# Two heads at a time: scores and values of a pair sent alternately in five attention stages

## What is computed

```python
rel = relu(einsum('bthd,bsd->bths', q_idx, k_idx)); score = einsum('bths,bth->bts', rel, w)   # index scores
logits = einsum('bthd,bshd->bhts', q, k) * scale        # DSA, MLA (qk over 64 + 32), MOBA, plus a bias or distance
logits = q @ k * scale + (c_q - c_k)                    # FOX, c = cumsum(log_sigmoid(f))
out = softmax(masked(logits)) @ v
# stick-breaking
z = q @ k * scale; log_1m = where(past, -softplus(z), 0)
w = where(past, exp(log_sigmoid(z) + reverse_exclusive_cumsum(log_1m)), 0); out = w @ v
```

## Time and profile before

| what | us |
| --- | --- |
| median of three runs | 1319.16 |
| lowest, highest | 1313.72, 1322.42 |
| span of the profiled execution | 1318.1 |
| PE busy | 1229.3 (93%) |
| POOL busy | 819.7 (62%) |
| ACT busy | 580.8 (44%) |
| DVE busy | 559.8 (42%) |

### The profile page before, as it was taken

One profiled execution on the slowest core, in us unless ns is written; L12 is line 12 of the kernel. 1 busy time (PEld: TensorE's weight loads), 2 busy tenths in 40 slices (PEclk: granted clock), 3 DMA queues, 4 the chain that ended last, 5 costly groups with the idle time before them and its releaser, 6 DMA issues.

```text
span 1318.1 us, 21658 instructions
## 1 busy us (share of the span) xinstructions
PE 1229.3 (93%) x8127; PEld 1083.5 (82%) x8127; DVE 559.8 (42%) x1133; ACT 580.8 (44%) x868; POOL 819.7 (62%) x286
## 2 busy tenths in 40 slices
PE   6898887999998879989999998999999998999996
PEld 2898686999996765779999968878899997899995
DVE  4368576655558573466223372133211043311113
ACT  0442433554542432435444525344578452544442
POOL 2666345888884520468888835545465677788884
PEclk9898887999999885789999998899999999899998
DMA  9698266999994240468556522524444545466552
GB/s 345 227 321 249 67 214 216 317 307 305 309 302 161 71 127 0 134 202 267 178 181 186 175 86 75 159 66 127 128 129 129 158 154 168 151 187 188 183 185 78
DMA packets 253065, 237.66 MB, mean 180 GB/s; under 512 B 17979, under 2 KB 216368, under 8 KB 253008
## 3 DMA queue, kind: packets, MB, share of 16 engines
q1 hardware_dynamic: 237312, 202.80, 49.6%
q10 hardware_dynamic: 14784, 31.98, 6.8%
q0 software_dynamic: 912, 2.09, 0.4%
HBM read 235.79 MB, written 1.05 MB: 180 GB/s over the span
## 4 chain that ended last, share of the span: by engine, by line
PE 74%; DVE 10%; DMA 5%; ACT 4%; POOL 4%; issue 2%; SPq 0%; DVEq 0%; POOLq 0%; ACTq 0%
PE bank L1125 17%; PE bank L1126 17%; PE bank L1127 17%; POOL unit_lo L679 3%; PE bank L1150 3%; PE bank L1152 2%; PE bank L1164 2%; PE bank L1277 2%; PE bank L1299 2%; ACT unit_hi L781 2%; DMA raw<-in_ev_w_in 2%; PE bank L1291 1%; PE bank L1196 1%; DVE x L1682 1%; PE bank L1280 1%
## 5 line engine op out<-in xcount | busy, mean ns | idle before, releaser
L679 POOL TENSOR_TENSOR unit_lo<-raw,unit_hi 128x2048 fp32r<-128x2048 f32 (+4 forms) x88 | 348.5, 3962 | 322.3 <-ACT unit_hi L781 322.2
L1125 PE MATMUL bank<-h_hi,unit_hi 128*128 128x256 f32 x1248 | 353.6, 283 | 0.0
L1126 PE MATMUL bank<-h_lo,unit_hi 128*128 128x256 f32 x1248 | 353.1, 283 | 0.0
L1127 PE MATMUL bank<-h_hi,unit_lo 128*128 128x256 f32 x1248 | 353.1, 283 | 0.0
L713 POOL TENSOR_TENSOR unit_lo<-raw,unit_hi 128x2048 fp32r<-128x2048 f32 (+1 forms) x70 | 257.3, 3675 | 85.8 <-ACT unit_hi L904 70.6
L1125 PEld LDWEIGHTS bank<-h_hi,unit_hi 128*128 128x128 f32 x1248 | 239.2, 192 | 4.1 <-issue 1.4
L1126 PEld LDWEIGHTS bank<-h_lo,unit_hi 128*128 128x128 f32 x1248 | 239.2, 192 | 2.7
L1127 PEld LDWEIGHTS bank<-h_hi,unit_lo 128*128 128x128 f32 x1248 | 239.2, 192 | 0.0
L781 ACT ACTIVATE unit_hi<-raw 128x2048 fp32r<-128x2048 f32 (+4 forms) x98 | 163.1, 1664 | 99.5 <-PE bank L1127 42.2
L716 POOL TENSOR_TENSOR down<-raw_down,down 128x1024 fp32r<-128x1024 f32 x70 | 168.4, 2406 | 0.0
L1789 DVE SCALAR_TENSOR_TENSOR work<-bank,cols,work 128x254 f32<-128x254 f32 (+1 forms) x176 | 72.7, 475 | 171.8 <-ACT work L891 171.8
(11 more groups left out here) (302 smaller groups left out, 2200.1 us busy)
## 6 DMA issues: line engine op xcount, KB each, us to landing
raw<-in_ffn_w_up SPq DMA_DIRECT2D x88, 512.0 KB, 5.2
raw<-in_w_in SPq DMA_DIRECT2D x60, 512.0 KB, 4.7
raw_down<-in_ffn_w_down SPq DMA_DIRECT2D x44, 512.0 KB, 4.9
raw<-in_w_up SPq DMA_DIRECT2D x64, 256.0 KB, 3.1
raw_down<-in_w_down SPq DMA_DIRECT2D x32, 512.0 KB, 3.5
raw<-in_ev_w_in SPq DMA_DIRECT2D x28, 512.0 KB, 5.2
ada<-in_ada_w ACTq DMA_DIRECT2D x13, 1024.0 KB, 6.6
att<-in_ada_w SPq DMA_DIRECT2D x12, 1024.0 KB, 7.7
```

What stands on the lines that cost most here:

```text
L679: nc.gpsimd.tensor_tensor(ul[g % 2][:, w], raw[g % 2][:, w], uh[g % 2][:, w].bitcast(F32), ALU.subtract).then_inc(lo_up, 1)
L1125: nc.tensor.matmul(o, sh, mh, start=first, stop=False)
L1126: nc.tensor.matmul(o, sh, ml, start=False, stop=False)
L1127: return nc.tensor.matmul(o, sl, mh, start=False, stop=last)
```

## The change

The ten steps over heads become four steps over pairs, in the index scores, the four softmax attentions and stick-breaking, on PE, ACT and DVE alike. `scores` sends the 128-column product of both heads, then the 256-column product of both; the rotary and bias products follow after those, alternately too. `weighted` sends the first product of both heads, then the second of both. Fillers are spread by `halves`: before the transposes of a pair and between the transposes and the values. Index scores use four banks instead of three. No product, no copy and no load is added or dropped.

```diff
-            turn(("idx", h), h % 3)
+            turn(("idx", h), h % 4)
...
+        FILL = {DSA: [[(G_BG[0], 0), (G_BG[0], 1)], [(G_BG[1], 0)], [(G_BG[1], 1)], [], [], [], [], []],
+                MLA: [[(None, 0), (None, 1)], [], [], [], [], [], [], []],
+                FOX: halves(G_QKV[MOBA], (3, 1, 2, 1, 2, 1, 1, 1)), MOBA: halves(G_QKVS, (3, 1, 2, 1, 2, 1, 1, 1)),
+                "stick": halves(G_GATE[:10], (3, 2, 3, 2, 3, 2, 3, 2))}
+
+        DONE = {a: [[g for g, part in fill if part == 1] for fill in f] for a, f in FILL.items()}
+        DONE[DSA] = [[], [], [G_BG[0]], [], [G_BG[1]], [], [], []]
+        DONE[MLA] = [[], [], [0, 1], [], [2], [], [3], []]
...
+                for h in range(4):
+                    exps(a, h)
+                for g in DONE[a][0]:
+                    filler(g)
+                for p in range(PAIRS):
+                    for h in (2 * p, 2 * p + 1):
+                        evac_pt(a, h)
+                    for g in DONE[a][2 * p + 1]:
                         filler(g)
+                    if p:
+                        out_high(a, p - 1)
+                    if p + 2 < PAIRS:
+                        for h in (2 * p + 4, 2 * p + 5):
+                            exps(a, h)
+                    if p + 1 < PAIRS:
+                        for g in DONE[a][2 * p + 2]:
+                            filler(g)
...
+            def scores(a, p):
+
+                heads = (2 * p, 2 * p + 1)
+                o = [begin(("score", a, h)) for h in heads]
+                q, k = qT(ATT_SET[a])[:, p, :], kT(ATT_SET[a])[:, p, :]
+                one = a in (DSA, MOBA)
                 for tt, (c0, n) in enumerate(((0, P), (P, S))):
...
+                    for i in range(2):
+                        r = slice(DH * i, DH * (i + 1))
+                        mm = nc.tensor.matmul(o[i][:, c0:c0 + n], q[r, P * tt:P * (tt + 1)], k[r, 0:n],
+                                              start=one or tt == 0, stop=one)
...
+                for tt, (c0, n) in enumerate(((0, P), (P, S)) if not one else ()):
+                    for i, h in enumerate(heads):
+                        if a == MLA:
+                            r0 = D_ROPE * (h % 4)
+                            mm = nc.tensor.matmul(o[i][:, c0:c0 + n], qrT[r0:r0 + D_ROPE, h // 4, P * tt:P * (tt + 1)],
...
+            def weighted(a, p, t, set_):
+
+                o, v = begin(("pv", a, p)), vv(set_)
+                for i in range(2):
+                    nc.tensor.matmul(o[DH * i:DH * (i + 1), 0:S], v[:, 0, DH * (2 * p + i):DH * (2 * p + i + 1)], t[i][:, 0:S],
+                                     start=True, stop=False)
+                for i in range(2):
...
+                scores(a, 0)
+                scores(a, 1)
+                for p in range(PAIRS):
+                    for g, part in FILL[a][2 * p]:
                         filler(g, part)
+                    for h in (2 * p, 2 * p + 1):
+                        transpose_p(a, h)
+                    for g, part in FILL[a][2 * p + 1]:
+                        filler(g, part)
...
+                    for h in (2 * p, 2 * p + 1):
+                        evacuated(pe, ("tr", a, h))
+                    weighted(a, p, PT, ATT_SET[a])
+                    if p + 2 < PAIRS:
+                        scores(a, p + 2)
...
+                for h in range(4):
+                    soft(a, h)
+                for h in range(2):
+                    normalize(a, h)
+                for p in range(PAIRS):
+                    for h in (2 * p + 2, 2 * p + 3) if p + 1 < PAIRS else ():
+                        normalize(a, h)
+                    for h in (2 * p + 4, 2 * p + 5) if p + 2 < PAIRS else ():
+                        soft(a, h)
+                    if p:
+                        out_low(a, p - 1)
                     if between:
```

More of the change, by code:

```diff
@@ L461, in leave, with halves @@
                 self.base, self.k = self.start + iterations * per, 0
[L464 to L473, removed]
+        PAIRS = HEADS // 2
+        def halves(units_, counts):
+            parts = iter([(g, part) for g in units_ for part in range(2)])
+            return [[next(parts) for _ in range(n)] for n in counts]
+        FILL = {DSA: [[(G_BG[0], 0), (G_BG[0], 1)], [(G_BG[1], 0)], [(G_BG[1], 1)], [], [], [], [], []],
[5 more added lines that the diff above has]
+        DONE[MLA] = [[], [], [0, 1], [], [2], [], [3], []]
         MOD_PE = (2, 3)
@@ L854, in attention @@
             def attention(a, filler):
[L855 to L862, removed]
-                        filler(g)
-                out_high(a, HEADS // 2 - 1)
+                for h in range(4):
[6 more added lines that the diff above has]
+                    for g in DONE[a][2 * p + 1]:
+                        filler(g)
+                    if p:
[6 more added lines that the diff above has]
+                            filler(g)
+                out_high(a, PAIRS - 1)
             def load_rows(a, *srcs):
@@ L1943, in _, with dsa_between @@
             unit_evacuated(dve, G_CX[-1])
-            def dsa_between(st):
-                for g in DONE[DSA].get(st, []):
+            def dsa_between(p):
+                for g in G_BG[p:p + 1]:
                     i = g - G_BG[0]
@@ L2048, in _, with mla_between @@
             dve.wait_ge(lat_lo, 3)
-            def mla_between(st):
-                i = st % 2
-                if st in (2, 3):
+            def mla_between(p):
+                for i in range(2) if p == 0 else ():
                     dve.wait_ge(pool_mixed, i + 1)
@@ L2061, in mla_between @@
                     ins.then_inc(pool_scaled, 1)
-                if st in (4, 5):
+                for i in range(2) if p == 1 else ():
                     dve.wait_ge(pool_hi, i + 1)
@@ L2089, in _ @@
             attention(MOBA)
-            for st in range(HEADS + 2):
-                if st < HEADS:
-                    h = st
+            for p in range(PAIRS):
+                heads = (2 * p, 2 * p + 1)
+                for h in heads:
                     o = full(dve, ("z", h))
@@ L2108, in _ @@
                     V.tensor_tensor(wT[h % 2], zm[h % 2], o[:, 0:384], ALU.subtract).then_inc(free(("sfx", h)), 1)
-                if st >= 2 and st % 2 == 1:
-                    out_low("stick", (st - 2) // 2)
+                if p:
+                    out_low("stick", p - 1)
+            out_low("stick", PAIRS - 1)
             for c in range(4):
```

151 lines of the change are left out of this document (61 added, 90 removed).

## The result

The changed kernel takes 1270.85 us (median of four runs, 1265.59 to 1272.92) against 1319.44 for the kernel before in the same session; the ratio is 0.9612, 95% interval 0.9585 to 0.964. In a second session it took 1267.62 (ratio 0.959, 0.9574 to 0.9606). By the first ratio the time is 0.9612 x 1319.16 = 1268 us. Forecast were 1281, range 1270 to 1300, so the gain was larger than expected and the time just past the edge of the range; the interval of the ratio, 1264 to 1272 us, takes in that edge. The profiled executions differ by more, 1318.1 - 1263.5 = 54.6 us: the changed kernel's is the fastest of its four. The kernel before comes in two groups: of 19 later executions 7 took 1313.2 to 1315.6 us at a mean granted clock of 0.946 to 0.950, the other 12 took 1320.5 to 1325.1 at 0.937 to 0.941, so single profiles of it can differ by some 7 us.

The account below looks back on a forecast made before the run. PE, with 74% of the chain, was taken as the bound, in DSA and MLA also VectorE's and ScalarE's order. Terms 0 - 7.3 - 12.2 - 8.0 - 5.6 - 5.0 = -38.1 took 1319.2 to 1281 us, range 1270 to 1300.

Parts of the forecast that it names:

- The walk through ScalarE: DSA: ScalarE's late evacuations make PE wait 2.9 and 5.7 us; the stage ends at 166.2 against 173.5, -7.3 us.
- The forecast's cover: Index scores: PE's saved 0.85 us falls before a 4.84 us wait ended by VectorE's top-k chain; counted 0.
- MLA: MLA stage: pairs overlap, 32-row products too, with W waiting on ScalarE; ends at 532.7 against 544.9, -12.2 us.
- then the low clock as now: MLA: scores of pairs 0 and 1 take 2.07 us each at full clock, later ones 3.73 at the low clock.
- the last rival (0.06): More than forecast: DSA's waits shrink and MLA's clock rises, time below 1272 us; chance 0.06.
- FOX: FOX stage: scores save 4.2 us, values 3.2, a shorter low clock 0.6, waits 0; sum -8.0.
- The term of 0.6: Start of FOX: the low clock shortens a little, as scores before the first filler take 6.2 us, not 8.8; 0.6 us.
- MOBA: MOBA stage: scores save 2.4 us and values 3.2; sum -5.6.
- Stick-breaking: Stick-breaking stage: logits save 2.6 us, values 3.2, and PE waits 0.8 for the last pair's `unit_hi`; sum -5.0.
- ScalarE as the pacer of the full stages: Rival: each pair step of the three full stages is late by one `unit_hi`, +23 us, 1304; chance 0.13.
- heads overlap only when sent whole: Rival: alternating does not overlap, scores and values keep their price, about 8 us gained, 1311; chance 0.07.
- The other side, a falling clock: Rival: with partial-array products together the clock falls, 44 halves cost 2.4 us more each, +106, 1387; chance 0.04.

Follow-up runs that it names:

- a0: The changed kernel once more, without an edit, for a second profile; 1267.62 us.
- a5: The changed kernel with both 64-row products of one head, then of the other, then the 8-row or 32-row ones likewise; 1265.99 us.
- a6: The changed kernel with the value products of a pair sent head after head; 1268.24 us.
- b2: The kernel before with only the index scores by pairs of heads over four banks; 1319.54 us, ratio 0.9996.
- c1: The changed kernel with the score products of FOX's first two pairs sent twice each; 1289.33 us.
- c2: The changed kernel with FOX's first heads in the order 0, 2, 1, 3, equal shapes together on the same half; 1270.64 us.
- a1: The changed kernel, still by pairs, with score products sent head after head as in the kernel before; 1302.66 us, ratio 0.9881 to before.
- a2: The changed kernel with scores head after head within a pair, equal shapes grouped inside each head; 1285.45 us, ratio 0.9754.

## Why the prediction was right or wrong, point by point

Most of the 16.5 us by which the profiles differ beyond the forecast's 38.1 come from two steps of it. It took the low clock of MLA and FOX as given, where the level stayed up (5.6 and 4.5 us). And it counted FOX's bias products in full and the transposes at nothing (3.0 and 1.5 us).

**DSA: right.** Forecast -7.3, measured -6.8 (-7.1 in a0, -8 in a5 and a6). The walk through ScalarE held nearly to the instruction: waits of 2.9 and 5.7 us forecast, 2.67 and 5.17 measured.

**Index: right, by b2**, though the profile first seemed to say otherwise. The forecast's cover, that VectorE's chain ends the wait, was the thing to question: one operation of that chain was lengthened twelvefold by POOL, and in the changed kernel and its variants it was held in four profiles of ten.

**MLA: mechanism right, size wrong.** The 32-row products of a pair do overlap (0.85 for both heads, 1.71 for the pair), and the waits before the second and third W were 4.52 and 5.05 against 3.9 and 4.3 forecast. The step that failed is "then the low clock as now": the mixes (2.0 us instead of 4.0), the first values, the third pair's scores (1.7 instead of 3.7) and the transposes behind them ran at full clock (PE reached that wait 12.8 us into the stage and not 17.8), and of the 5.6 us missed, 4.4 had been gained by the second W. This was in the text as the last rival (0.06), with no row behind it that told when the clock falls. Three profiles with the same MLA instructions (the changed kernel, c1, c2) took 32.4 to 32.6 us; a0 took 34.7 at 0.70, with the low level until 9.5 us into the stage and not 0.5, so the gain here is 16 to 18 us. What keeps the level up in MLA was not tested by itself: in a1, with the scores in the old order, it fell again 4.0 us into the stage, in the changed kernel not before 17.5, behind the first long wait.

**FOX: two terms mis-sized.** The sum of the parts, from rows at full clock:

- Scores: 4.16 to 2.36 for two heads, 4 x 1.80 = 7.2; forecast 4.2. "These stay on the same rows for both heads, so I count them in full" (the bias products) took 0.62 for one, a figure that holds the change of shape on either side of it. Four together take 1.51, not 2.08; and the 64-row part costs 0.85, not 1.04.
- Values: 4 x (2 x 0.79 - 0.80) = 3.1; forecast 3.2.
- Transposes, forecast nothing: each cost 0.48 in front of the values, two together in front of a filler 0.58 (827.15 to 827.73), 4 x 0.38 = 1.5.
- Clock: before at 0.50 from 842.9 to about 853.1, 10 us at half rate, 5.1; now never; forecast 0.6.

7.2 + 3.1 + 1.5 + 5.1 = 16.9, as measured. The row of the kernel before that shows the level, and the row after it:

```profile
842.80:845.80 3.00, 3.00 (x7) 1.48 (x8) 1.41 (x6) 2.09 (x5) 3.00 (x1) 0.52 0.82 287
...
854.80:857.80 3.00, 3.00 (x21) 2.41 (x19) 0.00 (x0) 1.23 (x2) 0.00 (x0) 1.00 0.00 0
```

The term of 0.6 assumed that the clock falls as before and only the scores behind it are fewer; 5.1 is what it gave when the level did not fall, and 3.6 in a5 and a6. It was partly luck: no row of the kernel before told that the level would stay, and its own fall is not fixed either (FOX 67.4 and 65.9 us with the same instructions).

**MOBA: short by 2.1.** 2.4 + 3.1, nearly as forecast, 1.5 more for transposes if they gain as in FOX; 0.7 is not assigned.

**Stick-breaking: right within a microsecond.** Its waits were 0.36, 0.95 and 1.50 us, 2.8 in all, where the walk had 0.8.

**Rivals.** ScalarE as the pacer of the full stages did not come about: PE never waits in FOX and MOBA. That heads overlap only when sent whole is refuted, and so is its mirror, that they must alternate (a5, a6). The other side, a falling clock, had the sign reversed: with the halves side by side the level fell later or not at all. Of the signs named for being right, the pairs' 0.85 and the values' 0.8 held; the second W of MLA waited 4.5 us where 3 to 4 were named, stick-breaking took 76.0 us for 75 with one wait of 1.5, and FOX near 59 (50.5), MLA near 38 (32.5), MOBA near 46.5 (44.3) and the wait of 5.7 before `cx` (1.32 and 4.66) did not hold.

## What to carry to other kernels

Take the price of a product from a row in which its neighbours have the shape that they will have: a bias product of this kernel took 0.52 us on average between other shapes and 0.38 among its own. Short products on opposite parts of the array need only stand next to each other. Look at the granted clock row by row, since more than half of what the profile of this change gained beyond the forecast was a level that stayed up, and take more than one profile before you credit it to an edit. Before trusting a long VectorE operation in a trace, look at what POOL does in the same microseconds; shorter GpSimd instructions gave 1% on a kernel in which nothing else was touched.

## What the runs showed of the hardware

- The 64-row products of two heads take 0.85 us, in both orders tried (0 1 0 1 and 0 0 1 1), and those of one head take 0.85 too (822.27 to 823.12 in a2), all at the full clock. 32-row products on different rows do the same: 0.85 for two heads in the changed kernel, 0.84 for one in a2 (501.74 to 502.58).
- Products alternating between 64 and 8 rows take 2.08 us a head, the same four grouped by shape 1.70: 0.19 for each of two changes saved (FOX at full clock).
- While PE was never idle, its granted clock fell from 1.00 to 0.50 in FOX, 2.5 to 5.5 us into the stage, and stood there for 3.5 to 13.5 us, part of it with full units running. Identical instructions up to that point kept it in one execution and lost it in another (a0 and a6, 1.5 us in FOX), and lost it after 3.0 and 5.0 us in two others (before and b2).
- A GpSimd instruction of 4.6 us held VectorE operations of 0.29 and 0.43 us for 3.54 and 4.67. The change's own profile reached DSA 4.3 us earlier than a repetition of it; 3.3 of that is this hold, the rest the granted clock behind it.
